# Expert rows gathered into four buffers beside the weights, four tiles of the shared expert done in the expert stage, and a last stage in two halves

## The chip, the cores and the metric

The kernel runs on one core of one Trainium2 chip. Five engines run their own instruction streams and meet at semaphores: TensorE (PE; its weight loads are listed as PEld), VectorE (DVE), ScalarE (ACT), GpSimd (POOL) and SyncE (SP). Sixteen DMA engines move the data; SP, ACT and POOL issue their transfers. The metric is the device time of one execution in microseconds (us), lower is better.

## The reference, cut to what matters

Two layers of a mixed recurrent block come first, then one attention block with a mixture of experts. All of it is float32, with 1024 tokens of width 1024. The change lies in the last part, after attention:

```
def moe_ffn(h, ...):                                   # h (1024 tokens, 1024)
    scores = sigmoid(h @ w_router)                     # 64 experts, 8 chosen per token
    ...
    gate = gate / sum(gate) * 2.5
    routed = routed_experts(h, idx, gate, w_gate, w_up, w_down)
    shared = (silu(h @ ws_gate) * (h @ ws_up)) @ ws_down
    return routed + shared

def expert_block(tok_b, w_b, e):                       # 128 rows of one expert, sorted by expert
    xb = h[tok_b]
    y = (silu(xb @ w_gate[e]) * (xb @ w_up[e])) @ w_down[e]
    return y * w_b[:, None]                            # added to the tokens' rows
...
x = x + g2 * ffn_x
return rmsnorm(x, final_g)
```

## The kernel before

The program is a row of stages, each closed by a barrier of all engines: the two recurrent layers, attention and pooling, the projection out, a norm, then `route` (line 2866), `experts` (3132) and `combine` (3427). Only the last three are touched. A stage's instructions are written per engine, so the order on an engine is the order of the calls in its block, and everything between engines is a semaphore wait.

**route** picks the experts, writes the tokens' rows (1024 values and 64 gates each) to the DRAM tensor `hrow`, makes the index tables, and runs the shared expert: gate and up products into `aT`, then (L3127) the down product for eight tiles of 128 tokens, eight matmuls a tile, each tile copied by ACT (L2949) and stored by SP in the DRAM tensor `sum`.

**experts** goes over blocks of 128 rows of one expert. The list of blocks is cut into four streams; round i takes block i of each stream, so u is 0 to 3 and the block's number is j = 4i + u. Consecutive blocks of a stream often have the same expert, and then the table points the weights' gather out of bounds, and nothing is moved. Each block needs three gathers, issued by POOL: its rows into `x` (two buffers, `rows`, L3198), its gate and up weights of 2 MB into `gu` (four buffers, `gate_up`), its down weights of 1 MB into `wd` (four buffers, `down`; both issued at L3202). Ahead of each gather a small POOL instruction copies the index column (L3197, L3208, L3214), and `settled` makes POOL wait for it. Afterwards `add` (L3226) adds the block's 128 output rows to `sum` in DRAM; each add waits until the one before has landed. In its turn for block j POOL does: add of j-2, gate_up of j+4, rows of j+3, down of j+3, and this last waits for PE's down product of j-1.

PE does in its turn for block j: `turn_x` of j+1 (L3377, eight transposes of the rows), `turn_a` of j-1 (L3385), `gate_up` of j (L3396, 24 matmuls in split float32), `down` of j-1 (L3407 and L3409). ACT and DVE split rows and weights in high and low parts (L3259, L3265, L3276 on ACT, L3315, L3330, L3338 on DVE), ACT drains the output (L3282), and DVE's `pick` copies the block's row numbers for the add (L3324) once the add three blocks back has landed.

**combine** reads `sum` back in eight tiles. Per tile PE transposes it (L3505), DVE adds it to the residual `xT` (L3463), ACT squares (L3518), PE sums the squares with matmuls on ones (L3497), ACT takes Ln and Exp (L3521, L3522), each with a load of its table ahead, DVE multiplies (L3472), ACT multiplies with the gain in eight instructions (L3528), SP stores the tile of `out`. ACT begins only once `final_g` has landed. For the last tile DVE multiplies by both at once (L3478).

## Time and profile before

| what | value |
|---|---|
| time, median of 3 runs | 4442.16 us (4432.85 to 4447.27) |
| the profiled execution's own time | 4437.05 us |
| its span | 4435.3 us |
| busy share of the span: PE, DVE, ACT, POOL | 87%, 52%, 40%, 30% |
| expert stage | about 3316 to 4340 us |
| last stage | 4345.8 to 4435.3 us |

Times in the trace are microseconds from the start of the span. A line of the timeline gives start, duration, engine, source line, operation, output and inputs, the count of instructions merged, and in brackets the idle time just before on that engine and what ended it. The share of DMA is the mean busy share of the sixteen DMA engines; it can read a little over 1. PEclk is the granted clock of PE, where 1.00 is 2.4 GHz and 0.50 is 1.2 GHz. Busy shares over the whole span hide that each stage has a limit of its own, so the prediction reads stretches.

### The profile page before, as it was taken

The page shows a single profiled execution, that of the slowest core. Times are in us where ns is not written, and L with a number is a line of the kernel's source. Part 1 is how long each engine was busy: PE and PEld are TensorE (multiplying, and loading weights), DVE is VectorE, ACT ScalarE, POOL GpSimd, SP SyncE. Part 2 cuts the span into 40 slices and gives each one's busy share as a digit, 9 for nine tenths or more (in the row PEclk, how much of TensorE's full clock was granted, in tenths as well). Part 3 has the DMA queues.
Part 4 walks back from the last instruction along what each step waited for, and adds up shares of the span by engine and source line. Part 5 has one row for each costly group of instructions (what it writes and reads, how often), then busy time and mean ns, then how long its engine had stood idle before and what let it go on. Part 6 is the DMA issues. An engine that isn't in the chain of part 4 may idle for free. (4 is left out here: it accounts for less than half of the span.)

```text
span 4435.3 us, 79300 instructions
## 1 busy us (share of the span) xinstructions
PE 3848.8 (87%) x30764; PEld 2884.5 (65%) x30764; DVE 2305.9 (52%) x3135; ACT 1791.9 (40%) x2347; POOL 1316.5 (30%) x991
## 2 busy tenths in 40 slices
PE   6999888888896998979997988888788999999994
PEld 3888676666674887766665754546546767666663
DVE  3365554553663001744554651742337878777772
ACT  1111245442332111444442341632206777777764
POOL 2221113211332221221221320002005767766750
PEclk8999899888898999988997999998798999999996
DMA  6766324112423432332213311011319989899973
GB/s 217 231 219 195 124 87 149 65 51 83 132 96 109 142 123 85 124 126 84 65 45 124 131 58 36 1 41 38 111 52 330 285 257 307 257 324 323 288 207 98
DMA packets 268917, 645.23 MB, mean 145 GB/s; under 512 B 39664, under 2 KB 131440, under 8 KB 251760
## 3 DMA queue, kind: packets, MB, share of 16 engines
q1 hardware_dynamic: 203280, 311.06, 21.3%
...
## 5 line engine op out<-in xcount | busy, mean ns | idle before, releaser
L472 PE MATMUL ps<-s_proj_hS,s_proj_wS 128*128 128x512 f32 x3216 | 768.5, 401 | 63.0 <-POOL s_proj_wS L362 63.0
L472 PEld LDWEIGHTS ps<-s_proj_hS,s_proj_wS 128*128 128x128 f32 x3216 | 614.9, 192 | 212.7 <-ACT s_proj_wS L422 63.9
L3396 PE MATMUL ps<-s_exp_wS,exp_x 128*128 128x512 f32 x2208 | 541.7, 401 | 0.7 <-issue 0.2
L3396 PEld LDWEIGHTS ps<-s_exp_wS,exp_x 128*128 128x128 f32 x2208 | 410.4, 189 | 98.4 <-issue 4.9
L527 PE MATMUL ps<-gate_h,gate_w 128*128 128x512 f32 x1536 | 414.7, 421 | 36.6 <-PEq L155 19.3
L514 POOL TENSOR_TENSOR gate_w<-gate_raw,gate_w 128x512 fp32r<-128x512 f32 x128 | 186.2, 1457 | 822.2 <-ACT gate_w L508 821.4
L527 PEld LDWEIGHTS ps<-gate_h,gate_w 128*128 128x128 f32 x1536 | 294.0, 196 | 138.8 <-issue 52.1
L390 DVE COPY s_proj_o<-ps 128x512 f32<-128x512 f32 x66 | 45.6, 691 | 568.2 <-PE ps L472 568.2
L362 POOL TENSOR_TENSOR s_proj_wS<-s_proj_w,s_proj_wS 128x1024 fp32r<-128x1024 f32 x67 | 168.6, 2519 | 570.6 <-ACT s_proj_wS L422 570.6
L3330 DVE TENSOR_TENSOR s_exp_wS<-exp_gu,s_exp_wS 128x1024 fp32r<-128x1024 f32 x276 | 325.3, 1219 | 14.1 <-ACT s_exp_wS L3265 14.0
L3265 ACT ACTIVATE s_exp_wS<-exp_gu 128x1024 fp32r<-128x1024 f32 x276 | 286.1, 1067 | 33.3 <-DMA exp_gu<-in_w_gu_dram,s_exp_widx 18.4
L422 ACT ACTIVATE s_proj_wS<-s_proj_w 128x1024 fp32r<-128x1024 f32 x67 | 70.8, 1059 | 492.7 <-DVE s_proj_o L390 232.3
L3226 POOL DMA_INDIRECT sum<-keep_hT,s_exp_sidx x92 | 207.7, 2257 | 88.6 <-DVE s_exp_sidx L3324 35.2
L2133 POOL TENSOR_TENSOR s_mix_wS<-s_mix_w,s_mix_wS 128x1024 fp32r<-128x1024 f32 x64 | 159.3, 2490 | 238.8 <-ACT s_mix_wS L2149 238.8
L2270 PE MATMUL ps<-s_mix_yS,s_mix_wS 128*128 128x512 f32 x768 | 182.9, 399 | 34.9 <-DVE s_mix_yS L2215 34.8
L2270 PEld LDWEIGHTS ps<-s_mix_yS,s_mix_wS 128*128 128x128 f32 x768 | 146.6, 191 | 72.6 <-issue 41.7
L2285 PE MATMUL ps<-s_mix_mS,s_mix_wS 128*128 128x512 f32 x768 | 192.3, 407 | 0.5 <-DVE s_mix_mS L2211 0.5
L3282 ACT ACTIVATE keep_hT<-ps,s_exp_rg 128x1024 f32<-128x1024 f32 x92 | 102.7, 1116 | 196.6 <-PE ps L3409 183.5
L3315 DVE TENSOR_TENSOR exp_x<-ps,exp_x 128x1024 fp32r<-128x1024 f32 x92 | 112.7, 1225 | 129.1 <-ACT exp_x L3259 129.1
L3377 PEld LDWEIGHTS ps<-keep_eye,s_exp_x 128*128 128x128 f32 x736 | 85.4, 145 | 135.7 <-issue 107.7
L2285 PEld LDWEIGHTS ps<-s_mix_mS,s_mix_wS 128*128 128x128 f32 x768 | 144.3, 188 | 44.5 <-issue 9.6
L3377 PE MATMUL ps<-keep_eye,s_exp_x 128*128 128x128 f32 x736 | 100.2, 281 | 76.1 <-DMA s_exp_x<-hrow,s_exp_idx 64.4
...
## 6 DMA issues: line engine op xcount, KB each, us to landing
...
gate_raw<-in_w_in_dram SPq DMA_DIRECT2D x128, 256.0 KB, 3.1
...
```

The costliest lines, as they stand in the source:

```text
L362: pool.tensor_tensor(wS[:, b, 1], w[:, b], wS[:, b, 0], ALU.subtract).then_inc(lo_ready, 1)
L472: mm = pe.matmul(k.ps[:, 6 + half if last else 2 * b + half, :], wS[:, b, x, t, :], hS[:, y, t, half * HALF:(half + 1) * HALF], start=(t = ...
L514: pool.tensor_tensor(self.w[:, n % RING, 1], self.raw[:, n % 2], self.w[:, n % RING, 0], ALU.subtract).then_inc(self.split_low, 1)
L527: mm = pe.matmul(self.k.ps[:, self.banks[g // 2], :], weight[:, w, t - t0, :], self.k.hG[:, h, t, :], start=(t == 0 and w + h == 0), stop= ...
L2133: pool.tensor_tensor(wS[:, z % 2, 1], w[:, z % 2], wS[:, z % 2, 0], ALU.subtract).then_inc(lo_ready, 1)
L2270: mm = pe.matmul(k.ps[:, 2 * b + x // 4, :], wS[:, z % 2, u, x, :], yS[:, v, x, :], start=(x % 4 == 0 and u + v == 0), stop=(x % 4 == 3 an ...
L2285: mm = pe.matmul(k.ps[:, 4 + b, :], wS[:, z % 2, u, x, :], mS[:, v, x, :], start=(x == 0 and u + v == 0), stop=(x == KT - 1 and u == 1))
L3226: pool.indirect_dma_start(total, bass.IndirectOffsetOnAxis(ap=sidx[:, u:u + 1], axis=0), y[:, u % 2, :], None, compute_op=ALU.add).then_in ...
L3265: act.activation(wS[:, pr, 0], gu[u][:, 2 * pr:2 * pr + 2], ACT.Copy).then_inc(hi_ready, 1)
L3330: dve.tensor_tensor(wS[:, pr, 1], gu[u][:, 2 * pr:2 * pr + 2], wS[:, pr, 0], ALU.subtract).then_inc(lo_ready, 1)
L3377: tr = pe.transpose(k.ps[:, t // 4, (t % 4) * P:(t % 4 + 1) * P], x[:, u % 2, t * P:(t + 1) * P], k.eye[:])
L3396: mm = pe.matmul(k.ps[:, 2 if u % 2 == 0 else 6, :], xS[:, u % 2, h, 2 * pr + t, :], wS[:, pr, w, t, :], start=(pr == 0 and t == 0 and h + ...
```

## The change

In **route**, the shared expert's down product is done for four tiles only (`NEARLY`), and the rows' buffers are cleared here rather than at the start of the expert stage. Two tables become one, `tab`, that holds a block's row number and weight index side by side.

In **experts**, PE, ACT and SP do the other four tiles first (`shared`). `x` has four buffers. `block_in` copies both indices at once, waits for that one copy, and issues rows and gate and up weights of the same block; `down` needs no copy. POOL's turn for block j becomes: rows and gate_up of j+4, add of j-2, down of j+3.

In **combine**, squares are summed for four tiles into one bank, and Ln and Exp run once for each half of the tokens. DVE applies scale and gain in one instruction of 512 tokens, and the output is stored in sixteen pieces of 128 rows by 512 tokens. ACT no longer waits for `final_g`.

```diff
+        self.tab = self.keep("tab", [P, 2, P, 2], I32)
+        self.x = self.keep("x", [P, STREAMS, D + NE])
+        self.sa = self.keep("sa", [P, 2, T])
...
+NEARLY = 4
...
+        wgu = k.mix[:, NEARLY:NEARLY + 4].rearrange("p (m f) (t n) -> p m f t n", m=2, t=KT)
+        wd, aT = k.swd, k.sa
...
-            for i in range(NTT):
+            for i in range(NEARLY):
                 sp.wait_ge(d_taken, i + 1)
                 sp.dma_start(k.scratch["sum"][i * P:(i + 1) * P, :], acc[:, i]).then_inc(st_x, 16)
...
+            mine.mark(dve.memset(k.x[:], 0.0))
...
+            mine.do(dve.scalar_tensor_tensor(k.tab[:, 0, :, 0], k.ps[:, 1, 0:NBLK], -1.0, same[:], ALU.add, ALU.add))
+            mine.mark(dve.tensor_copy(k.tab[:, 1, :, 0], k.tab[:, 0, :, 0]))
...
+            for n in range(NTT - NEARLY):
+                sp.wait_ge(late_taken, n + 1)
+                sp.dma_start(total[(NEARLY + n) * P:(NEARLY + n + 1) * P, :], late[:, n]).then_inc(st_late, 16)
             final = last_round(sp, k)
             wait(sp, lo_ready, final * (STREAMS * PR) + PR)
-            wait(sp, down_ready, final * STREAMS + 2)
             for t in range(KT):
+                if t in (4, 6):
+                    wait(sp, down_ready, final * STREAMS + (t // 2 - 1))
                 sp.dma_start(k.xT[:, t], k.scratch["x1"][t]).then_inc(ld_res, 16)
             sp.wait_ge(ld_res, 16 * KT)
...
-            pool.memset(none[:], 0).then_inc(none_ready, 1)
-            pool.wait_ge(none_ready, 1)
+            pool.reg_mov(freed, 1)
...
+            def fetch(dst, at, src, last, landed):
+                pool.indirect_dma_start(dst, None, src, bass.IndirectOffsetOnAxis(ap=at, axis=0), bounds_check=last, oob_is_err=False)\
+                    .then_inc(landed, 16)
+
+            def block_in(i, u, starts):
+                wait(pool, lo_ready, i * (STREAMS * PR) + (PR * (u + 1) - STREAMS * PR))
+                wait(pool, picked, i * STREAMS + (u + 1 - STREAMS))
+                wait(pool, ld_wd[u], i * 16, 16)
+                pool.tensor_copy(now[:, u], k.tab[:, 0 if isinstance(i, int) and i == 0 else 1, bass.ds(i + starts[u], 1), :]
+                                 .rearrange("p b n -> p (b n)")).then_inc(idx_ready, 1)
                 pool.reg_mov(copied, following)
                 pool.wait_ge(idx_ready, copied)
                 pool.reg_add(following, copied, 1)
-
-            def rows(i, u, starts):
-                wait(pool, ld_x[u % 2], i * (8 * STREAMS) + 16 * (u // 2), 16)
-                wait(pool, xtr_ready, i * STREAMS + (u - 1))
-                wait(pool, picked, i * STREAMS + (u - 1))
-                settled(pool.tensor_copy(idx[:, u % 2:u % 2 + 1], k.idx[:, bass.ds(i + starts[u], 1)]))
-                pool.indirect_dma_start(x[:, u % 2, :], None, hrow, bass.IndirectOffsetOnAxis(ap=idx[:, u % 2:u % 2 + 1], axis=0),
-                                        bounds_check=tokens, oob_is_err=False).then_inc(ld_x[u % 2], 16)
-
-            def fetch(dst, at, src, landed):
-                pool.indirect_dma_start(dst, None, src, bass.IndirectOffsetOnAxis(ap=at, axis=0), bounds_check=bound, oob_is_err=False)\
-                    .then_inc(landed, 16)
-
-            def gate_up(i, u, starts):
-                wait(pool, ld_gu[u], i * 16, 16)
-                wait(pool, lo_ready, i * (STREAMS * PR) + (PR * (u + 1) - STREAMS * PR))
-                settled(pool.tensor_copy(widx[:, u:u + 1], k.widx[:, 0 if isinstance(i, int) and i == 0 else 1, bass.ds(i + starts[u], 1)]))
-                fetch(gu[u][:].rearrange("p k n -> p (k n)"), widx[:, u:u + 1], w_gu, ld_gu[u])
-
-            def down(i, u, starts):
-                wait(pool, ld_wd[u], i * 16, 16)
-                wait(pool, down_ready, i * STREAMS + (u + 1 - STREAMS))
-                settled(pool.tensor_tensor(didx[:, u:u + 1], widx[:, u:u + 1], none[:], ALU.add))
-                fetch(wd[u][:].rearrange("p f n -> p (f n)"), didx[:, u:u + 1], w_down, ld_wd[u])
+                fetch(x[:, u], now[:, u, 0:1], hrow, tokens, ld_x[u])
+                fetch(gu[u][:].rearrange("p k n -> p (k n)"), now[:, u, 1:2], w_gu, bound, ld_gu[u])
+
+            def down(i, u):
+                if not (isinstance(i, int) and i == 0):
+                    pool.reg_mov(wanted, freed)
+                    pool.wait_ge(down_ready, wanted)
+                    pool.reg_add(freed, wanted, 1)
+                fetch(wd[u][:].rearrange("p f n -> p (f n)"), now[:, u, 1:2], w_down, bound, ld_wd[u])
...
+                if first(i, u):
+                    pool.wait_ge(st_late, 16 * (NTT - NEARLY))
+                else:
                     pool.wait_ge(st_y, prior)
                     pool.reg_add(added, prior, 16)
                 pool.indirect_dma_start(total, bass.IndirectOffsetOnAxis(ap=sidx[:, u:u + 1], axis=0), y[:, u % 2, :], None,
...
-                    pool.wait_ge(x_clear, 1)
-                    rows(0, 0, starts)
-                    gate_up(0, 0, starts)
-                    rows(0, 1, starts)
-                    for u in range(1, STREAMS):
-                        gate_up(0, u, starts)
-                        down(0, u - 1, starts)
-                    rows(0, 2, starts)
+                    for u in range(STREAMS):
+                        block_in(0, u, starts)
+                        if u < STREAMS - 1:
+                            down(0, u)
                 for u in range(STREAMS):
+                    if not last:
+                        block_in(i + 1, u, starts)
                     if not (isinstance(i, int) and i * STREAMS + u < 2):
                         add(*after(i - 1, u, STREAMS - 2))
-                    if not last:
-                        gate_up(i + 1, u, starts)
                     if not (last and u):
-                        rows(*after(i, u, 3), starts)
-                    if not (last and u):
-                        down(*after(i, u, 3), starts)
+                        down(*after(i, u, 3))
             add(i, STREAMS - 2)
             add(i, STREAMS - 1)
...
+            def shared(n):
+                act.wait_ge(late_ready, n + 1)
+                act.activation(late[:, n], banks(k, 4 + 2 * (n % 2)), ACT.Copy).then_inc(late_taken, 1)
+
+            shared(0)
+            shared(1)
+            shared(2)
+            rows_high(0, 0, 0)
             high(0, 0, 0, 0)
-            rows_high(0, 0, 0)
-            for pr in range(1, PR):
+            high(0, 0, 0, 1)
+            shared(3)
+            act.wait_ge(st_late, 16 * (NTT - NEARLY))
+            for pr in range(2, PR):
                 high(0, 0, 0, pr)
...
-            dve.memset(x[:], 0.0).then_inc(x_clear, 1)
-            low(0, 0, 0)
             rows_low(0, 0)
-            for pr in range(1, PR):
+            for pr in range(PR):
                 low(0, 0, pr)
...
-            turn_x(0, 0, 0)
+            def shared(n):
+                if n >= 2:
+                    pe.wait_ge(late_taken, n - 1)
+                for half in range(2):
+                    for f in range(2):
+                        mm = pe.matmul(k.ps[:, 4 + 2 * (n % 2) + half, :], k.sa[:, f, (NEARLY + n) * P:(NEARLY + n + 1) * P],
+                                       k.swd[:, f, half * HALF:(half + 1) * HALF], start=(f == 0), stop=(f == 1))
+                mm.then_inc(late_ready, 1)
+
+            for n in range(NTT - NEARLY):
+                if n == NTT - NEARLY - 1:
+                    turn_x(0, 0, 0)
+                shared(n)
+            pe.wait_ge(late_taken, NTT - NEARLY)
...
+            for h in range(2):
+                for t in range(KT):
+                    sp.wait_ge(o_ready, h * KT + t + 1)
+                    sp.dma_start(k.out[t, :, tokens(h)], o[:, t, tokens(h)]).then_inc(st_o, 16)
+            sp.wait_ge(st_o, 16 * 2 * KT)
...
-            for i in range(NTT):
-                if i:
-                    to_residual(i - 1)
-                if i >= 2:
-                    scaled(i - 2)
+            def gained(h, a, b):
+                dve.wait_ge(rstd_ready, h + 1)
+                dve.wait_ge(ld_g, 16)
+                dve.wait_ge(x_ready, (h + 1) * NH)
+                for t in range(a, b):
+                    dve.scalar_tensor_tensor(o[:, t, tokens(h)], k.xT[:, t, tokens(h)], fg[:, t:t + 1], rstd[:, h],
+                                             ALU.mult, ALU.mult).then_inc(o_ready, 1)
+
+            for i in range(NTT - 1):
+                to_residual(i)
+            gained(0, 0, KT // 2)
             to_residual(NTT - 1)
-            scaled(NTT - 2)
-            scaled(NTT - 1)
+            gained(0, KT // 2, KT)
+            gained(1, 0, KT)
...
-                wait(pe, rstd_ready, i - 1)
                 for t in range(KT):
-                    mm = pe.matmul(k.ps[:, 4 + i % 2, 0:P], k.ones[:], sq[:, i % 2, t], start=(t == 0), stop=(t == KT - 1))
+                    mm = pe.matmul(k.ps[:, 4 + i // NH, (i % NH) * P:(i % NH + 1) * P], k.ones[:], sq[:, i % 2, t],
+                                   start=(t == 0), stop=(t == KT - 1))
                 mm.then_inc(ss_ready, 1)
...
+
+            def deviation(h):
+                act.wait_ge(ss_ready, (h + 1) * NH)
+                act.activation(rstd[:, h], k.ps[:, 4 + h, :], ACT.Ln, scale=1.0 / D, bias=EPS).then_inc(ln_ready, 1)
+                act.wait_ge(ln_ready, h + 1)
+                act.activation(rstd[:, h], rstd[:, h], ACT.Exp, scale=-0.5).then_inc(rstd_ready, 1)
+
+            for i in range(NH + 1):
+                squares(i)
+            deviation(0)
+            for i in range(NH + 1, NTT):
+                squares(i)
+            deviation(1)
```

On POOL, in the steady part of the expert stage, a turn read before, from one add to the next:

```order
L3226 DMA sum<-keep_hT,s_exp_sidx 1152x1024
L3208 ISA
L3208 COPY s_exp_widx<-keep_widx 128x1
L3191 REGISTER_ALU
L3202 DMA s_exp_gu<-in_w_gu_dram,s_exp_widx 128x4096
L3197 ISA
L3197 COPY s_exp_idx<-keep_idx 128x1
L3191 REGISTER_ALU
L3198 DMA s_exp_x<-hrow,s_exp_idx 128x1088
L3214 TENSOR_TENSOR s_exp_didx<-s_exp_widx,s_exp_none 128x1
L3191 REGISTER_ALU
L3202 DMA s_exp_wd<-in_w_down_dram,s_exp_didx 128x2048
```

and now, the turn of the same kind (`s_exp_now` holds both indices, `keep_x` the rows):

```order
L3231 DMA sum<-keep_hT,s_exp_sidx 1152x1024
L3217 REGISTER_ALU
L3198 DMA exp_wd_23489<-in_w_down_dram,s_exp_now 128x2048
L3205 ISA
L3205 COPY s_exp_now<-keep_tab 128x2
L3209 REGISTER_ALU
L3198 DMA keep_x<-hrow,s_exp_now 128x1088
L3198 DMA exp_gu_23488<-in_w_gu_dram,s_exp_now 128x4096
L3230 REGISTER_ALU
```

One index copy is left of three, the rows go out ahead of the gate and up weights, and the add comes behind both.

On PE, from the end of route into the expert stage, before (L3127 is the shared down product, L3377 the transposes of a block's rows, L3396 its gate and up product):

```order
L3127 MATMUL ps<-s_route_wd,s_route_aT 128x512 x32
L153 UNCONDITIONAL_BRANCH
L3370 UNCONDITIONAL_BRANCH
L3377 MATMUL ps<-keep_eye,s_exp_x 128x128 x8
L2847 TENSOR_LOAD keep_nr
L2847 ISA x2
L3377 MATMUL ps<-keep_eye,s_exp_x 128x128 x8
L3396 MATMUL ps<-s_exp_wS,exp_x 128x512 x24
```

and now (L3133 and L3426 are the shared down product, L3386 the transposes):

```order
L3133 MATMUL ps<-keep_swd,keep_sa 128x512 x16
L156 UNCONDITIONAL_BRANCH
L3379 UNCONDITIONAL_BRANCH
L3426 MATMUL ps<-keep_swd,keep_sa 128x512 x12
L3386 MATMUL ps<-keep_eye,keep_x 128x128 x8
L3426 MATMUL ps<-keep_swd,keep_sa 128x512 x4
```

Half of the shared product stands behind the barrier, around the first block's transposes.

On ACT, in the last stage, one tile and a half before:

```order
L3518 ACTIVATE keep_hT<-keep_xT 128x1024
L3521 ACT_TABLE_LOAD
L3521 ACTIVATE s_comb_rstd<-ps 128x128
L3522 ACT_TABLE_LOAD
L3522 ACTIVATE s_comb_rstd<-s_comb_rstd 128x128
L3528 ACTIVATE keep_hT<-keep_hT,s_comb_fg 128x128 x8
L3518 ACTIVATE keep_hT<-keep_xT 128x1024
```

and now, the whole stage:

```order
L3531 ACTIVATE keep_hT<-keep_xT 128x1024 x5
L3535 ACT_TABLE_LOAD
L3535 ACTIVATE s_comb_rstd<-ps 128x512
L3537 ACT_TABLE_LOAD
L3537 ACTIVATE s_comb_rstd<-s_comb_rstd 128x512
L3531 ACTIVATE keep_hT<-keep_xT 128x1024 x3
L3535 ACT_TABLE_LOAD
L3535 ACTIVATE s_comb_rstd<-ps 128x512
L3537 ACT_TABLE_LOAD
L3537 ACTIVATE s_comb_rstd<-s_comb_rstd 128x512
```

Sixteen table loads became four, and the gain left ACT.

## Rows read from the trace of the kernel before

**Rows 1.** Stretches: bounds, length, busy PE, PEld, DVE, ACT, POOL (count), PEclk, DMA share, GB/s.

```profile
3446.50:4281.40 834.90, 784.73 (x3433) 574.82 (x3432) 653.09 (x938) 597.87 (x781) 590.14 (x547) 1.00 0.91 288
3346.50:3356.30 9.80, 0.43 (x2) 0.43 (x3) 0.00 (x0) 0.00 (x0) 2.22 (x3) 0.54 1.01 430
3955.30:4066.60 111.30, 100.46 (x440) 72.87 (x440) 83.55 (x121) 77.07 (x101) 77.22 (x71) 1.00 1.02 370
```

**Rows 2.** Timeline of PE: the transposes that open two turns without a wait.

```profile
3377.89 1.04 PE L3377 MATMUL ps<-keep_eye,s_exp_x 128*128 128x128 f32 x8
...
3387.70 1.04 PE L3377 MATMUL ps<-keep_eye,s_exp_x 128*128 128x128 f32 x8
```

**Rows 3.** Waits from 3440 to 4280 us: us in total, times, longest.

```profile
DVE s_exp_sidx L3324 <- DMA sum<-keep_hT,s_exp_sidx: 76.5, 61, 2.3
...
PE ps L3377 <- DMA s_exp_x<-hrow,s_exp_idx: 38.0, 37, 2.3
```

**Rows 4.** Timeline of POOL, one turn among blocks that all need new weights.

```profile
4005.30 2.54 POOL L3226 DMA_INDIRECT sum<-keep_hT,s_exp_sidx  x1 [1.27 <-DVE s_exp_sidx L3324]
4007.29 1.36 POOL L3208 COPY s_exp_widx<-keep_widx 128x1 int32 x1
4009.45 1.24 POOL L3202 DMA_INDIRECT exp_gu<-in_w_gu_dram,s_exp_widx  x1 [0.81 <-POOL s_exp_widx L3208]
...
4012.56 1.01 POOL L3198 DMA_INDIRECT s_exp_x<-hrow,s_exp_idx  x1 [0.79 <-POOL s_exp_idx L3197]
...
4015.96 2.37 POOL L3226 DMA_INDIRECT sum<-keep_hT,s_exp_sidx  x1 [0.35 <-issue]
```

**Rows 5.** Timeline of DVE beside Rows 4.

```profile
4006.26 3.49 DVE L3330 TENSOR_TENSOR s_exp_wS<-s_exp_gu,s_exp_wS 128x1024 fp32r<-128x1024 f32 x3
```

**Rows 6.** Timelines around the start of the expert stage: PE, then POOL, then PE.

```profile
3283.45 27.73 PE L3127 MATMUL ps<-s_route_wd,s_route_aT 128*128 128x512 f32 x64 [1.13 <-DVE s_route_aT L2964]
...
3318.30 0.19 POOL L3197 COPY s_exp_idx<-keep_idx 128x1 int32<-128x1 int32 x1 [2.17 <-DVE s_exp_x L3340]
...
3321.72 1.03 POOL L3202 DMA_INDIRECT exp_gu<-in_w_gu_dram,s_exp_widx  x1 [0.85 <-POOL s_exp_widx L3208]
...
3355.87 1.97 PE L3377 MATMUL ps<-keep_eye,s_exp_x 128*128 128x128 f32 x8 [13.67 <-DMA s_exp_x<-hrow,s_exp_idx]
```

**Rows 7.** DMA from 4332 to 4345 us: packets, MB, busy share of 16 engines.

```profile
q0 software_dynamic: 144, 0.52, 26.5%
```

**Rows 8.** Stretch of 52 us at the start, as Rows 1.

```profile
3316.00:3368.10 52.10, 22.21 (x85) 17.62 (x86) 23.71 (x31) 17.18 (x20) 21.82 (x31) 0.67 0.88 361
```

**Rows 9.** Chain that ended last: the wait for `final_g` in the last stage.

```profile
4349.87 9.96 DMA s_comb_fg<-in_final_g_dram
```

**Rows 10.** Timeline of ACT in the last stage: one tile.

```profile
4402.12 1.04 ACT L3518 ACTIVATE keep_hT<-keep_xT 128x1024 f32<-128x1024 f32 x1
...
4407.03 0.28 ACT L3521 ACTIVATE s_comb_rstd<-ps 128x128 f32<-128x128 f32 x1 [2.57 <-PE ps L3497]
4407.32 1.28 ACT L3522 ACT_TABLE_LOAD   x1
...
4408.83 2.43 ACT L3528 ACTIVATE keep_hT<-keep_hT,s_comb_fg 128x128 f32<-128x128 f32 x8
...
4411.17 1.04 ACT L3518 ACTIVATE keep_hT<-keep_xT 128x1024 f32<-128x1024 f32 x1
```

**Rows 11.** Timelines of PE, then DVE, in the last stage.

```profile
4360.96 3.70 PE L3497 MATMUL ps<-keep_hT,keep_ones 128*128 128x128 f32 x16 [7.57 <-ACT keep_hT L3518]
...
4351.72 4.23 DVE L3463 SCALAR_TENSOR_TENSOR keep_xT<-ps,keep_cond,keep_xT 128x128 f32<-128x128 f32 x16 [25.70 <-PE ps L3505]
...
4426.94 2.19 DVE L3478 SCALAR_TENSOR_TENSOR keep_hT<-keep_xT,s_comb_fg,s_comb_rstd 128x128 f32<-128x128 f32 x8 [7.83 <-ACT s_comb_rstd L3522]
```

**Rows 12.** Stretch of the last stage, as Rows 1.

```profile
4403.30:4408.00 4.70, 4.70 (x22) 4.70 (x23) 0.00 (x0) 2.11 (x3) 0.00 (x0) 0.50 0.39 104
```

**Rows 13.** Timeline of DVE in route: the wait for the router, then one 512-wide instruction.

```profile
3177.31 0.69 DVE L2958 TENSOR_TENSOR s_route_bi<-s_route_sc,s_route_bias 128x512 f32<-128x512 f32 x1 [26.62 <-ACT s_route_sc L2931]
```

105 lines of the change are left out of this document (33 added, 72 removed).

## The prediction

> **What bounds the kernel now.** I read the stretches first, then PE's timeline, then the waits, and last the chain. Three places matter, and each has a limit of its own.
>
> The loop over blocks: a turn in which PE waits for nothing takes 9.81 us from one group of transposes to the next [rows 2]. The long stretch of [rows 1] holds 78 turns (POOL runs 7 instructions a turn, 547 in all), so PE alone would need 765.2 us, and 834.9 us were used: 69.7 us are lost. Of these 38.0 us stand as a direct wait of the transposes for the gathered rows [rows 3]; the rest follows from late rows or from DVE, which waits 76.5 us for landed adds [rows 3]. The reader is to see the second load beside it: the DMA engines are busy 0.91 of the stretch, 760 us, nearly as much as PE needs. In a run of blocks that all bring new weights the share is 1.02, and ten turns took 111.3 us, 11.13 each [rows 1]. There transfers set the pace, not the date at which a gather is issued.
>
> POOL is close behind. In [rows 4] a turn takes 10.66 us from add to add, nearly all of it work: the rows go out 7.3 us after the add, behind the weights' gather and two index copies with 0.8 us of waiting each.
>
> The start of the expert stage: PE ends the shared product at 3311.2, POOL is in its stage from 3316.1 (its copy at 3318.30 stands behind 2.17 us of waiting for DVE to clear the rows' buffers), its first weight gather goes out at 3321.72, 5.6 us later, and at 3355.87 PE has waited 13.67 us for the third block's rows [rows 6]. DMA is at 0.88 over these 52 us [rows 8].
>
> The last stage, 89.5 us to the end of the span: ACT waits for a 4 KB load until 4359.8 [rows 9], and then a tile takes 9.05 us on one chain (square, PE's sums, Ln, table, Exp, gain) [rows 10]. PE idles between, and its clock is granted at 1.2 GHz [rows 12].
>
> **The start.** Half of 27.73 us leaves route: 13.9 us. The first weight gather then stands behind one copy (0.2 us), its wait (0.8) and the rows' issue (1.0), so 2.0 us after the stage's start and no longer 5.6, 3.6 us saved: the clearing of the buffers went to route, where DVE waits 26.62 us [rows 13]. Together the queue starts 17.5 us earlier. The four tiles' product now lies beside the first transfers, where PE had nothing to do; if that cover were gone it would cost its 13.9 us again. But their stores, 2.1 MB, join a queue that is the limit here; at 430 GB/s [rows 1] that is 4.9 us. ACT also waits for these stores before it splits the second half of the first weights, and behind it queue the splits that PE's first product waits for. PE crosses the barrier idle for some 4.9 us (3311.2 to 3316.1), and may run the four tiles at half clock, up to 4 us more, mostly under the gathers. That gives 17.5 - 4.9 = 12.6; I take **12 us**. Bounds: 5 if ACT's wait and the clock come on top, 23 if the 12% of idle DMA time of [rows 8] is used as well. That gain holds only while the queue is the limit up to about block 11, since PE, which waits less at first, soon meets the same transfers.
>
> **The loop.** The rows of a block leave three turns ahead of their use and in front of the 2 MB, not two turns ahead behind them. The direct wait of 38.0 us should go wherever DMA isn't full. Two copies with their waits leave POOL, about 2 x 1.0 to 2 x 2.1 us of its 10.66, so POOL falls below 9 us and is no bound. But bytes stay the same. What is late next is DMA itself in runs of new experts, and after that the add: POOL now issues it behind rows and weights, some 2 to 3 us later in PE's turn, and 2.1 MB (4.9 us at 430 GB/s) go in ahead of it, while one add alone keeps the engines busy for 3.4 us (26.5% of 13 us) [rows 7]. Queued behind POOL's wait for the last add is only the down gather of j+3, with four turns to spare; but DVE's copy of the row numbers waits for the add three back, and behind that copy on DVE stand the low parts that PE needs. So the gain is between 45 (all but the share that DMA keeps) and -10. Ten of 78 turns lose 13 us in one full run, and shorter runs do the same, so more than half of the 38 us is transport. I take 40% of it, **16 us**.
>
> Here a row and a rule are to be weighed. POOL's copy of 1.36 us ends at 4008.65 [rows 4], and the second of DVE's three L3330, which read two tiles in SBUF, ends at about 4008.6 [rows 5]; alone such a copy takes 0.19 [rows 6]. The Trainium skill, "SBUF — State Buffer" (SBUF: two separate sides), says that a GpSimd instruction that reads SBUF is blocked for the whole of a VectorE instruction with two SBUF inputs. By that rule the one remaining copy, which comes right after a down gather when DVE waits or works on PSUM, takes 0.2 us, and the loop would gain some 20 us; if it still took 1.4 as in [rows 4], the add would go out 1.2 us later, and some 8 us would be left.
>
> **The last stage.** First two tiles in the residual: 4351.72 + 4.23 = 4355.95, 10.1 us after the start [rows 11]; nothing waits for `final_g` by then. Six more tiles: transposes 1.04, as the same shape takes in [rows 2], sums 3.70 at 1.2 GHz [rows 11] or 1.85 at 2.4, and two handovers of 0.3: 3.5 to 5.3 each, 21 to 32. The first half's Ln, Exp and gain delay one square and one residual: 3. After the last tile: square 1.04, sums 1.9 to 3.7, Ln and Exp of 512 columns (not in the trace; 128 take 0.28 [rows 10], 1024 take 1.04, so 0.6 each), one table load 1.28, the other under PE: 5.5 to 7.2. Eight gains at 0.69, the 512-wide instruction of [rows 13]: 5.3. From DVE's last to the end 6.2 now (4429.1 to 4435.3); the last piece is half as large: 4.6 to 6.2. The sum is 50 to 64. I take 52.5, near the fast clock, since PE hardly idles between tiles any more. 89.5 - 52.5 = **37 us**, bounds 26 and 40.
>
> Other edits (one table, registers, the later loads of `xT` in three steps) lie under other engines' work: nothing.
>
> **Sum.** 12 + 16 + 37 = 65 us. The profiled execution took 4437.05, 1.8 more than its span, which stays: 4372. The median of the three runs is 5 us above it, so the forecast is 4377 us.
>
> **The rivals.**
> 1. The loop keeps its pace. For it: share 0.91 and 1.02 [rows 1]; the wait for rows turns into one for adds or weights. Against: where DMA has gaps nothing else is late. 12 + 0 + 37 = 49: 4393 us.
> 2. Gaps of both loads fall together, and four buffers level them: the loop nears 9.81 us a turn, gain 42. Total 91: 4351 us.
> 3. The add becomes the bound, and the kernel is slower. Place: DVE's copy and POOL's wait for the last add; price: x us in each of 78 turns, from x = (12 + 37)/78 = 0.63 on the kernel loses. For it: 76.5 us of such waits already [rows 3], and the add moved behind 4.9 us of weights. Against: DVE works 653.1/78 = 8.4 us a turn [rows 1], so it has 1.4 us of slack in 9.81, and in a turn of a repeated expert no weights stand ahead of the add. At 0.9 us a turn: 4442 - 49 + 70 = 4463 us. A milder form, 0.1 to 0.5 us a turn, gives 4401 to 4432. The Trainium skill, "DMA: Bandwidth & Descriptors" (Two DMAs through the same engine are not ordered), says that descriptors of one queue start in order but are pipelined: that would put the add fully behind the weights, as in this rival; no row shows the order within the queue.
> 4. The change gives the last stage little: PE stays at 1.2 GHz throughout: 26 in place of 37, 4388 us, inside the forecast's own range.
>
> **How the numbers follow.** Forecast 0.45 (own range 4362 to 4390), rival 1 0.22, rival 2 0.13, rival 3 0.12 (mild 0.09, slower 0.03), rival 4 alone with the rest 0.08. About 0.3% (13 us) is what a measurement of this kernel can tell from no change. Slower by more: 0.03. Within: 0.03, the worst of the mild form. Faster: 0.94. The range from 4348 to 4410 takes in rivals 1, 2 and 4 and the better part of the mild form, and leaves out about 0.15.
>
> **What would show it.** Expert stage starts near 3302 and no wait of 13 us in its first turns. In the loop: direct waits for rows near zero; if DMA is the limit, turns of new experts stay at 11.1 us with share 1.0, and repeated ones fall to 9.8. POOL idle some 2 us a turn. DVE's wait for adds at or above 76 us points to rival 3. Last stage: four table loads and 50 to 64 us in length. The forecast is wrong if the loop's total changes by more than 30 us either way, or if the last stage stays above 70.

## The result, and the profile after

The changed kernel takes 4500.95 us in the median of four runs (4493.93 to 4505.07); the kernel before took 4440.95 us beside it. The ratio is 1.0134, with a 95% interval from 1.0112 to 1.0157: slower by 1.3%, where 4377 us and "faster" were forecast. The profiled execution has a span of 4495.6 us against 4435.3 us, 60.3 us more. Three differences of time stamps make up that sum: the start of the expert stage gained 16 us, the last stage gained 42 us, and the loop between them lost 119 us; what lies before, between and behind them adds up to less than 1 us.

The waits of the changed kernel from 3440 to 4280 us, the view and stretch of [rows 3] (us in total, times, longest):

```profile
DVE s_exp_sidx L3335 <- DMA sum<-keep_hT,s_exp_sidx: 135.1, 42, 5.9
...
POOL sum L3231 <- DVE s_exp_sidx L3335: 92.7, 25, 5.1
PE ps L3416 <- DVE exp_dS L3349: 92.5, 27, 4.8
POOL s_exp_wd L3198 <- PE ps L3418: 85.2, 28, 5.7
POOL exp_wd L3198 <- PE ps L3418: 66.7, 23, 5.6
```

The direct wait of PE for rows, 38.0 us in [rows 3], has gone, as it should. In its place PE waits 92.5 us for DVE's low part of the down weights, and in fewer and longer pieces: 27 waits of up to 4.8 us. DVE's wait for landed adds has grown from 76.5 to 135.1 us, and its pieces from at most 2.3 to 5.9 us. Three of these rows make a chain: DVE waits for an add, PE for DVE, and POOL's down gather for PE; behind the down gather, in POOL's order, comes a later add. The row that puts POOL's add down to DVE's copy is no link of it. By the code an add waits for its own block's row numbers, which were copied three turns before, and for the landing of the add before it, the same landing that DVE's copy had just waited for.

The stretch of [rows 1] and PE's two groups of the down product in the changed kernel from 3440 to 4280 us (count | busy, mean ns | idle before):

```profile
3446.50:4281.40 834.90, 742.11 (x3077) 545.70 (x3076) 584.82 (x841) 526.65 (x700) 419.96 (x350) 0.93 0.85 259
```

```profile
L3416 PE MATMUL ps<-exp_dS,s_exp_aS 128*128 128x512 f32 x420 | 138.2, 475 | 92.5 <-DVE exp_dS L3349 92.5
L3418 PE MATMUL ps<-exp_wd,s_exp_aT 128*128 128x512 f32 x144 | 77.7, 666 | 0.0
L3418 PE MATMUL ps<-s_exp_wd,s_exp_aT 128*128 128x512 f32 x136 | 75.4, 683 | 0.0
```

And the same product in the kernel before:

```profile
L3407 PE MATMUL ps<-s_exp_dS,s_exp_aS 128*128 128x512 f32 x474 | 123.8, 396 | 7.8 <-DVE s_exp_dS L3338 7.4
L3409 PE MATMUL ps<-exp_wd,s_exp_aT 128*128 128x512 f32 x160 | 75.1, 592 | 0.0
L3409 PE MATMUL ps<-s_exp_wd,s_exp_aT 128*128 128x512 f32 x156 | 73.2, 592 | 0.0
```

POOL runs 350 instructions where it ran 547, the DMA share has fallen from 0.91 to 0.85, and PE's granted clock from 1.00 to 0.93. The clock has a price that stands in the busy column: at the 123.8/474 = 0.261 us of the kernel before, the 420 matmuls of L3416 would have kept PE busy for 109.7 us and not 138.2, and at its 0.469 us the two groups of L3418 for 67.6 and 63.8 and not 77.7 and 75.4. That is 28.5 + 10.1 + 11.6 = 50 us. PE's timeline says the same: in 25 of 70 turns the down product took 4.5 to 6.1 us up to the next transposes, in the others 3.1. So of what PE lost in this stretch 92.5 us are waits, and some 50 us are the matmuls right behind the waits, at a lower clock.

One bad turn and one good one, timelines of POOL, DVE and PE in the changed kernel (start us, us, operation, [idle before <-releaser]):

```profile
3990.57 2.59 POOL L3231 DMA_INDIRECT sum<-keep_hT,s_exp_sidx  x1 [0.30 <-issue]
3994.79 1.03 POOL L3198 DMA_INDIRECT s_exp_wd<-in_w_down_dram,s_exp_now  x1 [1.63 <-PE ps L3418]
3995.82 0.20 POOL L3205 COPY s_exp_now<-keep_tab 128x2 int32 x1
...
4004.21 2.39 POOL L3231 DMA_INDIRECT sum<-keep_hT,s_exp_sidx  x1 [5.06 <-DVE s_exp_sidx L3335]
4011.79 1.04 POOL L3198 DMA_INDIRECT s_exp_wd<-in_w_down_dram,s_exp_now  x1 [5.20 <-PE ps L3418]
4012.84 0.19 POOL L3205 COPY s_exp_now<-keep_tab 128x2 int32 x1
4013.82 1.02 POOL L3198 DMA_INDIRECT keep_x<-hrow,s_exp_now  x1 [0.79 <-POOL s_exp_now L3205]
4015.14 0.99 POOL L3198 DMA_INDIRECT exp_gu<-in_w_gu_dram,s_exp_now  x1 [0.30 <-DVE s_exp_sidx L3335]
4016.43 2.58 POOL L3231 DMA_INDIRECT sum<-keep_hT,s_exp_sidx  x1 [0.30 <-issue]
```

```profile
4003.46 0.15 DVE L3335 COPY s_exp_sidx<-keep_tab 128x1 int32 x1 [5.79 <-DMA sum<-keep_hT,s_exp_sidx]
...
4003.90 1.22 DVE L3349 TENSOR_TENSOR exp_dS<-s_exp_wd,exp_dS 128x1024 fp32r<-128x1024 f32 x1
```

```profile
3990.71 1.56 PE L3416 MATMUL ps<-exp_dS,s_exp_aS 128*128 128x512 f32 x6
3992.11 1.88 PE L3418 MATMUL ps<-s_exp_wd,s_exp_aT 128*128 128x512 f32 x4
...
4005.26 2.90 PE L3416 MATMUL ps<-exp_dS,s_exp_aS 128*128 128x512 f32 x6 [4.60 <-DVE exp_dS L3349]
4007.96 3.04 PE L3418 MATMUL ps<-s_exp_wd,s_exp_aT 128*128 128x512 f32 x4
```

The reader is to follow one add. It is issued at 3990.57. DVE's wait for it ends at 4003.46, 12.9 us later; in the kernel before the median from issue to landing is 9.1 us (row below). DVE copies and makes dS until 4005.1, PE runs the down product from 4005.26 to 4011.0 (at 1.2 GHz: 2.90 and 3.04 us, where 1.56 and 1.88 stand at 2.4 GHz), POOL's down gather has waited 5.20 us for it and goes at 4011.79, and behind it, in POOL's fixed order, come the copy, the rows, the weights, and at 4016.43 the next add but one. That ring takes 4016.43 - 3990.57 = 25.9 us and spans two turns of the loop: 12.9 us a turn, against 9.81 for PE alone. In the trace a turn of 9.8 us often stands between two of 14 to 18 us.

This is one of the longest rings. Counted from the landing events of the traces, from 3410 to 4280 us, the changed kernel's 72 adds landed 6.1 to 12.9 us after their issue, 9.9 in the median, 16 of them after more than 12 us; the 82 adds of the kernel before took 6.3 to 11.4 us, 9.1 in the median. So the late landing is only a part of it. Another part is POOL's own: from the end of its down gather to the add it takes 4016.43 - 4012.83 = 3.6 us for copy, rows and weights, which the kernel before has behind its add. The third is PE's clock, some 2.5 us.

```profile
sum<-keep_hT,s_exp_sidx POOLq DMA_INDIRECT x82, 9.1
```

The last stage, 47.4 us from 4448.2 us on (bounds, then columns as in [rows 1]); ACT's table loads and DVE's last gains stand below it:

```profile
4448.20:4495.60 47.40, 26.33 (x192) 24.84 (x192) 27.86 (x80) 15.93 (x16) 0.00 (x0) 0.79 0.47 178
```

```profile
4481.34 1.06 ACT L3531 ACTIVATE keep_hT<-keep_xT 128x1024 f32<-128x1024 f32 x1 [3.74 <-DVE keep_xT L3487]
4482.42 1.28 ACT L3535 ACT_TABLE_LOAD   x1
4484.54 0.60 ACT L3535 ACTIVATE s_comb_rstd<-ps 128x512 f32<-128x512 f32 x1 [0.84 <-PE ps L3511]
4485.15 1.28 ACT L3537 ACT_TABLE_LOAD   x1
...
4487.11 5.39 DVE L3496 SCALAR_TENSOR_TENSOR keep_mix<-keep_xT,s_comb_fg,s_comb_rstd 128x512 f32<-128x512 f32 x8 [3.16 <-ACT s_comb_rstd L3537]
```

The start, timelines of PE and POOL, to set beside [rows 6]:

```profile
3282.05 14.00 PE L3133 MATMUL ps<-keep_swd,keep_sa 128*128 128x512 f32 x32 [1.13 <-DVE keep_sa L2968]
...
3301.82 0.18 POOL L3205 COPY s_exp_now<-keep_tab 128x2 int32<-128x2 int32 x1 [197.26 <-issue]
...
3338.09 1.04 PE L3386 MATMUL ps<-keep_eye,keep_x 128*128 128x128 f32 x8
```

And one row of the waits from 3290 to 3420 us, ACT's for the late stores:

```profile
ACT s_exp_wS L3266 <- DMA sum<-keep_hT: 11.5, 1, 11.5
```

From the beginning of the shared product to the third block's transposes it took 3355.87 - 3283.45 = 72.4 us [rows 6], and now 3338.09 - 3282.05 = 56.0 us: 16.4 us gained, and the wait of 13.67 us is gone.

### The profile page after: what moved, and what is told of

It reads as the page before. It is cut to its first block and busy times, and to the rows that moved or that the text cites. A ratio compares the mean times of both kernels' runs of the same rounds, so it can differ in the third digit from the quotient of the medians.

```text
span 4495.6 us, 78378 instructions
## 1 busy us (share of the span) xinstructions
PE 3888.8 (87%) x30764; PEld 2911.5 (65%) x30764; DVE 2304.3 (51%) x3137; ACT 1749.1 (39%) x2267; POOL 1190.2 (26%) x806
## 5 line engine op out<-in xcount | busy, mean ns | idle before, releaser
L3266 ACT ACTIVATE s_exp_wS<-exp_gu 128x1024 fp32r<-128x1024 f32 x276 | 282.8, 1068 | 17.5 <-DMA sum<-keep_hT 11.5
L3416 PE MATMUL ps<-exp_dS,s_exp_aS 128*128 128x512 f32 x552 | 181.2, 474 | 119.8 <-DVE exp_dS L3349 119.8
L3231 POOL DMA_INDIRECT sum<-keep_hT,s_exp_sidx x92 | 217.2, 2360 | 179.7 <-DVE s_exp_sidx L3335 118.6
L3416 PEld LDWEIGHTS ps<-exp_dS,s_exp_aS 128*128 128x128 f32 x552 | 122.0, 227 | 160.1 <-issue 133.3
```

Source lines behind the costliest of these rows:

```text
L3231: pool.indirect_dma_start(total, bass.IndirectOffsetOnAxis(ap=sidx[:, u:u + 1], axis=0), y[:, u % 2, :], None, compute_op=ALU.add).then_in ...
L3266: act.activation(wS[:, pr, 0], gu[u][:, 2 * pr:2 * pr + 2], ACT.Copy).then_inc(hi_ready, 1)
L3416: pe.matmul(k.ps[:, 4 + half, :], aS[:, h, :], dS[:, w, half * HALF:(half + 1) * HALF], start=(h + w == 0), stop=False)
```

## The experiments

**Theory A**: the loss is the place of the add in POOL's single queue. Behind the rows and 2 MB of weights it lands late, DVE waits for it in order, and PE waits for DVE. Later it took the sharper form C, the ring of two turns. **Rivals**: B, the rows' transfers themselves, sent four turns early; C', POOL running far ahead with fewer copies; and A2, POOL's own wait of each add for the one before, rather than DVE's. (In the expectations "Theory C" is the ring, and "Rival C" what is called C' here.)

To compare single executions I use a number that leaves the start and the last stage out: from the transposes of the third block to those of the last, 89 turns, which are 873 us at 9.81 each. What is above 873 is the loop's loss. Kernels with the same loop show what the column can tell: 73.7 and 70.4 (before, e4), 52, 53 and 53 (e2, e8, e9), 15 and 18 (e6, e10). Each is a single execution, and single runs of the kernel before lie between 4419 and 4447 us, so small differences in this column say nothing. Times of different groups of runs are compared by their ratio to the kernel before.

| kernel | us, median | ratio to before (95%) | loop's loss, us |
|---|---|---|---|
| before | 4436 to 4441 | 1 | 74 |
| changed | 4500.95 | 1.0134 (1.0112 to 1.0157) | 193 |
| e1 changed, add first | 4375.05 | 0.9856 (0.9838 to 0.9874) | 73 |
| e2 changed, add between | 4355.04 | 0.9813 (0.9797 to 0.9829) | 52 |
| e3 before, add behind weights | 4505.98 | 1.0156 (1.0139 to 1.0173) | 142 |
| e4 before, new last stage | 4393.28 | 0.9908 (0.9892 to 0.9925) | 70 |
| e5 changed, numbers two turns later | 4349.24 | 0.9798 (0.9776 to 0.9821) | 44 |
| e12 changed, numbers one turn later | 4346.82 | 0.9804 (0.9779 to 0.9829) | 44 |
| e6 = e2 + numbers two turns later | 4321.62 | 0.9740 (0.9724 to 0.9756) | 15 |
| e7 = e1 + numbers two turns later | 4331.47 | 0.9766 (0.9739 to 0.9793) | 34 |
| e8 = e2 + late stores' wait moved | 4345.95 | 0.9797 (0.9780 to 0.9814) | 53 |
| e9 = e2, no late shared product | 4364.65 | 0.9830 (0.9812 to 0.9849) | 53 |
| e10 = e6 + e8 | 4319.11 | 0.9741 (0.9720 to 0.9762) | 18 |
| e11 before, numbers two turns later | 4434.50 | 0.9996 (0.9981 to 1.0011) | 77 |

### The place of the add: e1, e2, e3

e1, in the changed kernel:

```diff
                 for u in range(STREAMS):
+                    if not (isinstance(i, int) and i * STREAMS + u < 2):
+                        add(*after(i - 1, u, STREAMS - 2))
                     if not last:
                         block_in(i + 1, u, starts)
-                    if not (isinstance(i, int) and i * STREAMS + u < 2):
-                        add(*after(i - 1, u, STREAMS - 2))
```

> The changed kernel with one thing put back: in each turn POOL issues the add of block j-2 ahead of rows and gate/up weights of block j+4, as the kernel before did; four row buffers, one index copy, late shared product and the new last stage stay. Theory A (the place of the add in POOL's single queue costs the time: behind some 2.6 MB it lands 13.3 us after its issue, DVE's in-order copy of the row numbers waits for it, PE's down product comes late and at half clock): the add lands again in 8 to 10 us, DVE's wait for it falls from 146.6 us to under 80, and the kernel needs 4441 - 18 (start) - 42 (last stage) - 0 to 20 (waits for rows) = 4361 to 4381 us. Rival B (the rows sent ahead of the weights and four turns early press on the DMA queue whatever the add does): it stays at 4470 to 4500. Rival C (fewer index copies let POOL run so far ahead that the down weights collide): 4440 to 4480.

Measured 4375.05 us. One pair of statements exchanged brings back 126 us. The waits, 3440 to 4280 us:

```profile
DVE s_exp_sidx L3335 <- DMA sum<-keep_hT,s_exp_sidx: 89.3, 44, 4.3
PE ps L3416 <- DVE exp_dS L3349: 29.4, 30, 2.7
```

Rivals B and C' are out: rows are still sent four turns early and ahead of the weights, and POOL still has one copy. The total hit its expectation, but the size given for DVE's wait didn't: under 80 us were expected, 89.3 were seen (99.1 in the longer stretch from 3400 us that the expectation counts), more than the 76.5 of [rows 3]. That is the first sign that the add was near its limit before the change as well.

e2, in the changed kernel:

```diff
                 fetch(x[:, u], now[:, u, 0:1], hrow, tokens, ld_x[u])
-                fetch(gu[u][:].rearrange("p k n -> p (k n)"), now[:, u, 1:2], w_gu, bound, ld_gu[u])
+
+            def gate_up(u):
+                fetch(gu[u][:].rearrange("p k n -> p (k n)"), now[:, u, 1:2], w_gu, bound, ld_gu[u])
...
                     if not last:
                         block_in(i + 1, u, starts)
                     if not (isinstance(i, int) and i * STREAMS + u < 2):
                         add(*after(i - 1, u, STREAMS - 2))
+                    if not last:
+                        gate_up(u)
```

> The changed kernel with the add between the rows and the gate/up weights of block j+4: 0.5 MB stand ahead of it instead of 2.6 MB. Theory A: the wait grows with the bytes ahead, so nearly all comes back: landing at 9 to 11 us, 4370 to 4400 us. Rival B, in its narrow form (it is the rows' gather of 128 scattered pieces directly ahead of the add that holds it): 4450 or more. If the loss came from the order of POOL's waits instead of from bytes, this kernel is near the changed one too, 4480 to 4500.

Measured 4355.04 us, better than expected, and better than e1 (the intervals don't touch). So 0.5 MB ahead of the add cost nothing that shows. What went behind the add is two things at once: the 2 MB, and the 1.3 us that POOL takes to issue them. Adds land sooner than in the changed kernel (median 8.6 us, longest 11.6, against 9.9 and 12.9), but in e1, with nothing of the turn ahead of the add, they take 10.1 us in the median and up to 12.2, and that kernel is 126 us faster all the same. How much of the loss is the late landing and how much the later issue in POOL's order, no run separates. Why e2 beats e1 isn't separated either. In e1 POOL's copy of two numbers comes after the add, at a time when DVE works on SBUF tiles, and takes 1.36 us; in the changed kernel it comes after the down gather and takes 0.19. Both rows are from 3410 to 4280 us (duration ns min/median/max), e1 first:

```profile
L3205 POOL COPY s_exp_now<-keep_tab x80: 742/1360/1772, 3417.9 to 4255.3; 128x2 int32 x80
```

```profile
L3205 POOL COPY s_exp_now<-keep_tab x73: 182/190/203, 3415.0 to 4276.4; 128x2 int32 x73
```

e3, in the kernel before:

```diff
                 for u in range(STREAMS):
+                    if not last:
+                        gate_up(i + 1, u, starts)
                     if not (isinstance(i, int) and i * STREAMS + u < 2):
                         add(*after(i - 1, u, STREAMS - 2))
-                    if not last:
-                        gate_up(i + 1, u, starts)
```

> The kernel before with one thing changed: the add of block j-2 goes out behind the gate/up weights of block j+4 (still ahead of the rows); two row buffers, three index copies, old start and old last stage. Theory A: the same loss without the rest of the change, +60 to +110 us, 4500 to 4550 us, with adds landing some 12 to 13 us after issue and DVE's waits for them above 130 us in place of 76.5. Rivals B and C: no more than +20 us, 4441 to 4460.

Measured 4505.98 us, 70 us slower than before and within its range; DVE's waits are a little shorter than the 130 us expected. The waits, 3440 to 4280 us:

```profile
DVE s_exp_sidx L3324 <- DMA sum<-keep_hT,s_exp_sidx: 122.4, 40, 5.4
...
PE ps L3407 <- DVE s_exp_dS L3338: 70.7, 35, 3.9
```

The same exchange in the old kernel makes a loss of the same kind with nothing else of the change there, 69 us in the loop where the changed kernel lost 119: cause and place are shown from both sides. Where the other 50 us come from isn't separated; here the rows still go out behind the add.

### Which wait carries it: e5, e12

e5, in the changed kernel, add still last. DVE's copy leaves `pick` and is made two turns later (POOL's guard of the shared buffer moves from `picked` to `eg_ready`):

```diff
-                wait(dve, st_y, i * (16 * STREAMS) + (16 * (u + 1) - 16 * STREAMS), 16)
-                dve.tensor_copy(sidx[:, u:u + 1], k.tab[:, 0, b, 0]).then_inc(picked, 1)
...
                         pick(j + 1, *after(i, u, 1), starts)
                     if not first(i, u):
+                        number(*after(i - 1, u, STREAMS - 1), starts)
                         turned(j - 1)
```

The new function `number` holds the two removed lines, here for block j-1. The guard wasn't moved alone in any run.

> The changed kernel, add still behind rows and gate/up weights, but DVE copies a block's row numbers two turns later: its copy then waits for an add that was issued three turns ago, not one. Theory A1 (DVE's in-order wait for a landed add is the link that holds PE): DVE's waits for adds go to nearly nothing, PE's waits of 101 us for DVE's dS go with them, and most of the 100 us come back: 4380 to 4420 us. Rival A2 (POOL's own wait, each add for the one before it, with rows and weights between, is a chain of about 13 us a turn by itself): the wait moves from DVE to POOL, ACT's output waits for the buffer instead, and the kernel stays at 4470 to 4505 us.

Measured 4349.24 us, 152 us under the changed kernel and under its own expectation. The waits, 3440 to 4280 us:

```profile
POOL sum L3231 <- DMA sum<-keep_hT,s_exp_sidx: 167.3, 44, 7.1
ACT keep_hT L3283 <- DMA sum<-keep_hT,s_exp_sidx: 90.8, 27, 4.8
...
PE ps L3420 <- DVE exp_dS L3351: 14.1, 20, 1.9
```

This is the row that decides. The wait for landed adds has not gone: POOL now waits 167.3 us for them, more than DVE did. But behind POOL's wait there stand only gathers with turns to spare, and behind ACT's wait a copy that PE needs late, while behind DVE's stood dS, which PE needs at once. Rival A2 is out. A2 had also counted some 13 us for every add. That is only the longest: in this run they land 5.9 to 12.9 us after their issue, 9 of 86 after more than 12 us, and the median is 8.7 us (issue to landing, 3410 to 4280 us):

```profile
sum<-keep_hT,s_exp_sidx POOLq DMA_INDIRECT x86, 8.7
```

e12 moves the copy by one turn only: `number(i, u, starts)` at the same place, and `number(0, 0, starts)` once ahead.

> The changed kernel, add behind rows and weights, with DVE's copy of the row numbers moved by one turn only (it waits for the add issued two turns ago). Theory C (a closed ring of waits that spans two turns: add issued, landed 12.9 us later, DVE's copy and dS 1.8, PE's down product 5.7 at half clock, POOL's down gather, copy, rows, weights and the next add 5.4, together 25.9 us, or 12.9 a turn): one turn more in the ring makes three turns of at most 25.9, which is under 3 x 9.81 = 29.4 us, so the ring no longer binds and all comes back that came back with two turns: 4345 to 4360 us. Rival (each turn of delay takes away its share of the waits): half way between 4501 and 4349, 4410 to 4440 us.

Measured 4346.82 us: one turn gives all that two turns give. A delay that took away its share of the waits would have left 4410 us or more. It is the ring that binds or doesn't: 25.9 us are too much for two turns (19.6 us at PE's pace) and fit into three (29.4). That the ring closes through POOL's down gather is read from the timeline; the runs open it only at DVE's copy, and no run opens it at another link.

### The other parts: e4, e9, e8

e4 is the kernel before with the function `combine` of the changed one, and no other line.

> The kernel before with the last stage of the changed one alone. The trace of the changed kernel has this stage 42 us shorter (47.4 against 89.5): 4441 - 42 = 4399 us, 4396 to 4403. Rival: part of that was not the edit but what the expert stage leaves (PE's clock, the later loads of x): 4405 to 4415.

Measured 4393.28 us, a ratio of 0.9908: 41 us, with an interval of 33 to 48. What the new last stage gives, it gives alone. The time lies 3 us under the expected range, which started from 4441 us; the kernel before beside it took 4436.33.

e9, in e2: the late half goes back to route.

```diff
-NEARLY = 4
+NEARLY = 8
...
-            for n in range(NTT - NEARLY):
-                if n == NTT - NEARLY - 1:
-                    turn_x(0, 0, 0)
-                shared(n)
-            pe.wait_ge(late_taken, NTT - NEARLY)
+            turn_x(0, 0, 0)
```

> The kernel with the add between rows and weights, with all eight tiles of the shared down product back in the routing stage. The difference to 4355 us is what the late half brings. By the trace of the changed kernel, third block's transposes 18 to 19 us earlier: 4355 + 18 = 4373 us. If the loop's transfers take the early start back later, as they should where the queue is the limit: 4358 to 4365. Against the kernel before with the new last stage (4393 us), what is left is then the four row buffers, the one index copy and the order in the loop.

Measured 4364.65 us, 9.6 us above e2. The intervals of the two ratios overlap (0.9830 from 0.9812, 0.9813 to 0.9829), so this is a size and not a proof. It lies at the upper end of the second expectation, but not for its reason: the loop's loss is 52 and 53 us, so there is no sign that the loop takes the early start back. What was too high is the 18 us. From the beginning of the shared product to the third block's transposes e2 takes 55.9 us, and e9, with all eight tiles in route, 60.3:

```profile
3289.49 27.73 PE L3133 MATMUL ps<-keep_swd,keep_sa 128*128 128x512 f32 x64 [1.13 <-DVE keep_sa L2968]
...
3349.81 1.10 PE L3381 MATMUL ps<-keep_eye,keep_x 128*128 128x128 f32 x8 [0.99 <-DMA keep_x<-hrow,s_exp_now]
```

So the late half brings 4.4 us there; the 18 us had counted in what the other edits of the start give.

e8, in e2: ACT's wait for the late stores stands ahead of `output(0)` and no longer inside the first block's splits.

```diff
             shared(3)
-            act.wait_ge(st_late, 16 * (NTT - NEARLY))
...
+                    if isinstance(i, int) and j == 2:
+                        act.wait_ge(st_late, 16 * (NTT - NEARLY))
                     if not (isinstance(i, int) and j < 2):
                         output(j - 2, *after(i - 1, u, STREAMS - 2))
```

> The kernel with the add between rows and weights, with ACT's wait for the stores of the late shared tiles (10.9 us, between its second and third split of the first gate/up weights) put ahead of its first write of an output block instead. If that wait, which the prediction named as a bound of the start, is paid at the end: 4343 to 4351 us. If the first turns are paced by the DMA queue anyway, as the prediction took it: 4351 to 4358, no change.

Measured 4345.95 us, 9 us under e2 by the medians, again with overlapping intervals; the two groups' runs of the kernel before differ by 3 us. e10 below has the same edit on e6 and shows nothing in the time (0.9741 to 0.9740). The traces show where it acts: the third block's transposes come 51.4 us after the beginning of the shared product, where e2 has 55.9, and 52.5 in e10, where e6 has 55.9. So the wait holds the start up by 3 to 5 us; whether the whole kernel keeps them is undecided.

### What was left of it: e6, e7, e11, e10

e6 is e2 with e5's edit.

> The kernel with the add between rows and weights (4355 us), with DVE's copy of the row numbers two turns later. There DVE still waits 71.4 us for adds and PE 17.5 us for dS. If that wait is the remaining loss: 4338 to 4350 us. If DVE only waits in time it has to spare, within 4 us of 4355.

Measured 4321.62 us, more than the 5 to 17 us expected. From 3440 to 3860 us PE is never idle (bounds, columns as in [rows 1]), and in the run of blocks that all bring new weights the share of DMA is 1.02, and that is the limit left:

```profile
3440.00:3860.00 420.00, 420.00 (x1889) 318.66 (x1888) 362.96 (x514) 322.36 (x430) 255.81 (x216) 1.00 0.94 298
3860.00:3960.00 100.00, 98.63 (x440) 73.72 (x438) 84.42 (x120) 73.28 (x97) 51.96 (x46) 1.00 1.02 367
```

Turns outside that run take 9.8 us one after the other; in it they take 11.1, as in [rows 1].

> The kernel with the add first in the turn (4375 us), with DVE's copy two turns later. With the copy late, add last gave 4349 and add between 4322 us. If the place in the queue still counts by the bytes ahead of the add: 4312 to 4322 us. If what now counts is that POOL comes late with rows and weights after waiting for the last add: 4325 to 4345 us.

e7, the add first in the turn and the late copy, measured 4331.47 us, a ratio of 0.9766 (0.9739 to 0.9793), which overlaps e6's; the time lies in the second expectation, though its interval touches the first. With the copy out of the way the place of the add is worth at most some 28 us (e5 against e6), where it was worth 146 (the changed kernel against e2).

> The kernel before with DVE's copy of the row numbers two turns later and nothing else. Theory C: its ring of two turns is add to landing 9.1, DVE 1.8, PE 3.4, POOL's down gather 1.0 to 2, some 16 us, under 2 x 9.81, so it does not bind; what DVE waits (76.5 us) lies half beside PE's own work, and the waits for rows (38.0 us) stay: 4415 to 4435 us. If the ring bound here too, all of the 70 us that PE lost in the loop could go except the rows' 38: below 4415.

e11, e5's edit in the kernel before, measured 4434.50 us, at the upper end of what was expected: no change, ratio 0.9996 (0.9981 to 1.0011). The edit worth 152 us in the changed kernel is worth nothing in this one. Its waits, 3440 to 4280 us:

```profile
PE ps L3381 <- DMA s_exp_x<-hrow,s_exp_idx: 54.3, 41, 3.3
POOL sum L3226 <- DMA sum<-keep_hT,s_exp_sidx: 45.0, 27, 2.7
```

DVE's 76.5 us for adds are gone, and PE's wait for rows has grown from 38.0 to 54.3 us. In e1 it is the other way round: the waits for rows are gone, DVE's for adds have grown, and the loop's loss is 73 us, as before. The old loop had two limits of about the same height, and to take away either alone gives nothing. With both gone (e7, add first) the loss is 34 us.

> The changed kernel with three moves together: add between rows and weights, DVE's copy two turns later, ACT's wait for the late stores ahead of its first output block. If the gains add: 4322 - 9 = 4313 us, 4308 to 4318. If the start's 9 us are taken back once the loop runs at PE's pace of 9.8 us a turn: they are not, since PE is then the bound and an early start is kept; the rival is that the queue limits the first turns of new experts, then 4318 to 4324.

e10, all three moves in the changed kernel, measured 4319.11 us, ratio 0.9741 (0.9720 to 0.9762) and the same as e6: of the two expectations, the second by its number. That the queue takes the start back isn't shown; the loop's loss is 18 us against 15. e6 is the simpler one, and it beats both kernels: 2.6% under the kernel before and about 4% under the changed one.

## Why the prediction was wrong

**The start: right in its size, by other terms.** 12 us were forecast, with bounds 5 and 23, and the third block's transposes come 16.4 us earlier. The stage starts near 3302 and the wait of 13 us is gone, as the text said. But the sum was 13.9 us for the late half, less 4.9 for its stores, and 3.6 for the earlier first gather. By e9 the late half gives 4.4 us and not 9.0, and what is there without it gives 72.4 - 60.3 = 12.1 and not 3.6. That the two errors nearly cancel is luck. ACT's wait for the late stores is there, 11.5 us long, and holds the start up by 3 to 5 us (e8, e10).

**The last stage: right in its mechanism, off by 5 us.** 37 us were forecast, with bounds 26 and 40; 42 were seen in the trace, just outside them, and e4 gives 41 by the ratio. By terms, with the marks of the sum: the first two tiles are in the residual 9.8 us after the start (10.1), then 23.3 us pass until the last square (21 to 32, and 3 for the first half's Ln, Exp and gain), 5.8 us for the last deviation (5.5 to 7.2), 5.4 for eight gains (5.3), and 3.1 us from DVE's last to the end (4.6 to 6.2). The tail was mis-sized: the last stored piece is half as large as before, and 3.1 us is half of the 6.2 us seen there, where only a part was taken off. The middle lies just under its low end of 21 + 3: its 3 us were for the first half's work, and the trace has DVE's gains for that half between its tiles while PE went on.

**The loop: the step that failed.** Forecast was a gain of 16 us between +45 and -10; it lost 119. The change did what the text said it would: direct waits for rows went to zero, POOL's copy takes 0.19 us, and POOL's own work was no bound. (By the rule of the Trainium skill, "SBUF — State Buffer" (SBUF: two separate sides), that was the right value of the two, and e1 shows the other one, 1.36 us, when the copy stands elsewhere.) Rival 3 had the place, the price and the breakeven: DVE's copy, behind an add behind 2 MB of weights, and a loss from 0.63 us a turn. Measured were 119 / 89 = 1.34 us a turn. What failed is its chance of 0.12, 0.03 of it for slower, and three sentences behind that:

- "Queued behind POOL's wait for the last add is only the down gather of j+3, with four turns to spare". The down gather itself waits for PE's down product, and behind it in POOL's order stand the next turn's rows, weights and the next add. So the issue of an add is tied to PE's product, PE's product to DVE's dS, DVE's dS to the landing of an earlier add. Each link stood in the text; that they close a ring wasn't seen, and its length was never added up. From the trace of the kernel before it could have been: add to landing at 9.1 us and some 4 more for the weights (4.9 us by the text's own number), DVE 1.8, PE 3.4, and for POOL's down gather, copy with its wait, rows and weights 1.0 + 1.0 + 1.3 + 1.3. That is 23 us, or 11.5 a turn, above 9.81 before any clock is lost. (The trace has 12.0 a turn over the 89 turns, (873 + 193)/89. The 4 us more fit the longest landings, 12.9 us, and not the median, which rose by 0.8.)
- "DVE works 653.1/78 = 8.4 us a turn [rows 1], so it has 1.4 us of slack in 9.81". Mean slack of an engine says how late its work may come on the average. DVE's wait stood at one place in its order, directly ahead of the one thing that PE needed next. Slack later in the turn doesn't help there, which e5 and e12 show: the same DVE work, in another order, and 152 us.
- "in a turn of a repeated expert no weights stand ahead of the add." True, but the ring spans two turns, and one late add is enough to stall both.

**The clock** was missing in the loop's sum altogether: some 50 us of the loss are matmuls at a lower clock behind waits of 2.1 to 4.8 us. A stall was priced at its length, and cost about (92.5 + 50)/92.5 = 1.5 times that.

On the order within the queue, the Trainium skill, "DMA: Bandwidth & Descriptors" (Two DMAs through the same engine are not ordered), says that descriptors of one queue start in order and are pipelined. The traces agree with that as far as they go: issued behind the weights, adds took up to 12.9 us to land, 9.9 in the median, against 11.4 and 9.1 before. The text named this as what rival 3 needs, and left the rival at 0.12.

What would have been right with the add left in its place: 12 + 16 + 37 gave 4377, and e1 shows 4375. But the terms are others there (16, 0 and 42), so the match of the sums is chance. For the loop alone rival 1 ("the loop keeps its pace") describes e1, and rival 2 ("levelled near 9.81") describes e6, but only with the copy moved as well.

**Left open:** how much of the loss is the add's late landing and how much its later issue; why e2 is 20 us faster than e1 (the copy's 1.2 us, or rows that go out ahead of the add); and whether the kernel keeps the 3 to 5 us that ACT's wait costs at the start.
